# Decode attention in one step of a hybrid decoder: scores for two page groups per matmul, pages laid in pairs, a third sample's pages loaded in the stage before

## What is computed

```python
# 8 samples, 8 heads, 2048 past positions in 16 pages of 128; latent width 256, rotary width 32
ckv_past = cache_ckv[layer, page_table].reshape(b, -1, KV_LORA)
kpe_past = cache_kpe[layer, page_table].reshape(b, -1, QK_ROPE)
q_lat = jnp.einsum('bshd,chd->bshc', q_nope, p['w_uk'])
sc_past = jnp.einsum('bshc,btc->bhst', q_lat, ckv_past) + jnp.einsum('bshr,btr->bhst', q_pe, kpe_past)
...
pr = jax.nn.softmax(sc, axis=-1).astype(ckv.dtype)
o_lat = (jnp.einsum('bhst,btc->bshc', pr[..., :n_past], ckv_past)
         + jnp.einsum('bhst,btc->bshc', pr[..., n_past:], ckv))
return jnp.einsum('bshc,chd->bshd', o_lat, p['w_uv']).reshape(b, s, A_HEADS * V_DIM)
```

## Time and profile before

| what | value |
|---|---|
| three runs | 1036.63, 1037.03, 1031.61 us (median 1036.63) |
| profiled execution, first to last instruction | 1035.9 us |
| PE busy in it | 946.9 us |
| prompt attention block, decode attention block | about 217 to 255 us, about 255 to 338 us |
| granted TensorE clock, mean | 0.961 |

### The profile page before, as it was taken

One profiled execution on the slowest core, in us unless ns is written; L12 is line 12 of the kernel. 1 busy time (PEld: TensorE's weight loads), 2 busy tenths in 40 slices (PEclk: granted clock), 3 DMA queues, 4 the chain that ended last, 5 costly groups with the idle time before them and its releaser, 6 DMA issues. The chain is left out here.

```text
span 1035.9 us, 18712 instructions
## 1 busy us (share of the span) xinstructions
PE 946.9 (91%) x7761; PEld 583.3 (56%) x7761; DVE 340.8 (33%) x840; ACT 192.5 (19%) x461; POOL 120.2 (12%) x148
## 2 busy tenths in 40 slices
PE   4599999998998688999599999999999999999996
PEld 3488888876555456855554544454445454444451
DVE  0323660046344874525522322221121222212124
ACT  1010010325222591003111111110111111111102
POOL 0000000041563000000001101101011111101000
PEclk8899999998999787999889999999999999999998
DMA  9947575543796848076569999999999999999951
GB/s 376 318 173 289 206 313 204 204 164 128 255 346 215 344 172 347 11 280 256 222 222 405 426 421 419 417 420 418 398 405 423 420 423 421 421 421 398 401 196 50
DMA packets 56023, 319.87 MB, mean 309 GB/s; under 512 B 14929, under 2 KB 24738, under 8 KB 35010
## 3 DMA queue, kind: packets, MB, share of 16 engines
q1 hardware_dynamic: 43138, 300.20, 72.2%
q0 software_dynamic: 11072, 18.28, 5.2%
q10 hardware_dynamic: 1728, 0.18, 0.1%
HBM read 321.32 MB, written 15.77 MB: 325 GB/s over the span
## 5 line engine op out<-in xcount | busy, mean ns | idle before, releaser
L390 PE MATMUL bank<-h,ring 128*128 128x264 f32 x672 | 154.9, 391 | 9.7 <-PEq L306 9.1
L390 PEld LDWEIGHTS bank<-h,ring 128*128 128x128 f32 x672 | 128.1, 192 | 33.9 <-issue 12.2
L2315 DVE TENSOR_TENSOR hh<-sge,bank 64x256 f32<-64x256 f32 x64 | 27.1, 423 | 231.1 <-ACT sge L2226 231.1
L2226 ACT ACTIVATE sge<-bank 64x256 f32<-64x256 f32 x64 | 24.1, 377 | 416.7 <-PE bank L2108 416.7
L2108 PE MATMUL bank<-done_out,xt 128*64 128x256 f32 x832 | 95.6, 382 | 0.0
L2108 PE MATMUL bank<-ring,xt 128*64 128x256 f32 x800 | 94.9, 391 | 0.8 <-ACT xt L2217 0.8
L2262 DVE COPY sq<-bank 128x512 f32<-128x512 f32 x64 | 44.3, 692 | 110.7 <-PE bank L2049 107.5
L2049 PE MATMUL bank<-ring,ht 128*32 128x512 f32 x400 | 72.8, 598 | 3.2 <-DMA ring<-in_w_e 1.8
L1542 POOL DMA_INDIRECT xg<-tok_rows,tab_g x32 | 31.9, 998 | 375.2 <-PE bank L2035 342.5
L2108 PEld LDWEIGHTS bank<-done_out,xt 128*64 128x64 f32 x832 | 58.6, 138 | 27.1 <-issue 0.2
L2108 PEld LDWEIGHTS bank<-ring,xt 128*64 128x64 f32 x800 | 57.7, 142 | 28.6 <-issue 3.3
(11 more groups left out here) (462 smaller groups left out, 1194.7 us busy)
## 6 DMA issues: line engine op xcount, KB each, us to landing
ring<-in_w_units SPq DMA_DIRECT2D x28, 2048.0 KB, 10.6
done_out<-in_w_e SPq DMA_DIRECT2D x26, 2048.0 KB
ring<-in_w_e SPq DMA_DIRECT2D x25, 2048.0 KB
slot_b<-in_w_e SPq DMA_DIRECT2D x13, 2048.0 KB
ring<-in_w_e SPq DMA_DIRECT2D x25, 1024.0 KB
slot_b<-in_w_e SPq DMA_DIRECT2D x13, 1024.0 KB
done_out<-in_w_e SPq DMA_DIRECT2D x13, 1024.0 KB
row_of<-in_w_e SPq DMA_DIRECT2D x13, 1024.0 KB, 16.4
```

The lines of the kernel that those rows point to most:

```text
L390: mm = pe.matmul(bank[:, t % NB, 0:T], w[:, j, k, :], h[:, k, :], start=(k == 0), stop=(k == KD - 1))
L2226: act.activation(sg[e % 2][:, :], bank[0:LB, 4, 0:FE], ACT.Silu).then_inc(sg_ready, 1)
L2315: dve.tensor_tensor(hh[e % 2][:, :], sg[e % 2][:, :], bank[LB:2 * LB, 4, 0:FE], ALU.mult).then_inc(hh_ready, 1)
```

## The change

`held_turned` holds page 2 of samples 3 to 7 turned for m = 0 and 1 instead of m = 0 and 2. Two neighbouring groups make a pair. For each pair `score_pair` takes one matmul of 256 columns where `score_group` took two of 128; its moving operand spans both groups (a slice of two in the page buffer, or `page_t`, now laid out as 5 slots of a pair's two turned pages). TensorE's order becomes: turns of groups 0 and 1; turns of groups 2 and 3, scores of the first pair, `turn_weights` of sample b - 1; scores of the second pair; `weigh` of sample b - 1. VectorE takes all its copies of sample b before the probabilities of sample b - 1. In the prompt block `kh` now lies in `x`, and `val`, `t2` and `q_rows` in `sq`; with that memory free, SP and POOL issue the loads of three samples there (`range(NBUF)`) and begin with sample 3 in the decode block.

```diff
@@ -40,7 +40,7 @@
-    return g == 3 or (g == 2 and (b < FULL or m % 2 == 0))
+    return g == 3 or (g == 2 and (b < FULL or m < 2))
@@ -49,6 +49,13 @@
+PAIRS = {}
+for _b in range(TS):
+    for _h in range(NPG // 8):
+        for _g in range(4):
+            if not held_turned(_b, 2 * _h, _g):
+                PAIRS[_b, _h, _g] = len(PAIRS)
+NPAGE_T = 5
@@ -572,17 +579,19 @@
-    own = ExitStack()
-    kh = sb("kh", [QH, NH, TP], stack=own)
-    val = sb("val", [P, 2, NH * VD], stack=own)
+    page.append(page2)
+    rope.append(rope2)
+    kh = x[0:QH, :, 0:TP]
+    spare = sq[:, :, :].rearrange("p k t -> p (k t)")
+    val = spare[:, 0:2 * NH * VD].rearrange("p (t c) -> p t c", t=2)
...
-        t2 = sb("t2", [P, 2, T], stack=ph)
+        t2 = spare[:, 2 * NH * VD:2 * NH * VD + 2 * T].rearrange("p (a t) -> p a t", a=2)
...
-        q_rows, q_turned = sb("q_rows", [P, 2 * KVL], stack=ph), sem("q_turned", ph)
+        q_rows, q_turned = spare[:, 2 * NH * VD + 2 * T:2 * NH * VD + 2 * T + 2 * KVL], sem("q_turned", ph)
@@ -600,18 +609,19 @@
-                for b in range(NBUF - 1):
+                for b in range(NBUF):
...
-                for b in range(NBUF - 1):
+                for b in range(NBUF):
@@ -778,16 +788,8 @@
-    own.close()
...
-        page.append(page2)
-        rope.append(rope2)
-        page_t = early[:, 0:16 * P].rearrange("p (n i t) -> p n i t", n=8, i=2)
+        page_t = early[:, 0:4 * NPAGE_T * P].rearrange("p (s i m t) -> p s i m t", s=NPAGE_T, i=2, m=2)
@@ -827,7 +829,7 @@
-                for b in range(NBUF - 1, TS):
+                for b in range(NBUF, TS):
@@ -836,46 +838,51 @@
-                    pg = page[b % NBUF]
...
-                    for m in range(GR + 1):
-                        if m < GR:
...
-                        if b and m == 2:
+                    for h in range(GR // 2 + 1):
+                        if h < GR // 2:
+                            turn_pages(b, 2 * h)
+                            turn_pages(b, 2 * h + 1)
+                        if h >= 1:
+                            score_pair(b, h - 1)
+                        if b and h == 1:
...
-                def score_group(b, m):
-                    n = max(TURNS[b, m, g] for g in range(4) if not held_turned(b, m, g))
+                def turn_pages(b, m):
+                    pg = page[b % NBUF]
+                    pe.wait_ge(page_in[b % NBUF][m], 16 * 3 * (b // NBUF + 1))
+                    pe.wait_ge(fourth_in[b % NBUF][m], 16 * 2 * (b // NBUF + 1))
+                    for g in range(4):
+                        if held_turned(b, m, g):
+                            continue
+                        n = TURNS[b, m, g]
+                        if n >= 4:
+                            pe.wait_ge((turn_took_a, turn_took_d)[n % 2], (n - 4) // 2 + 1)
+                        for i in range(2):
+                            at = page_at(g) + i * P
+                            mm = pe.transpose(bank[:, n % 4, i * P:(i + 1) * P], pg[:, m, at:at + P], ident)
+                        mm.then_inc(turned, 1)
...
+                def score_pair(b, h):
+                    n = max(TURNS[b, 2 * h + 1, g] for g in range(4) if not held_turned(b, 2 * h + 1, g))
...
+                    ms, cols = slice(2 * h, 2 * h + 2), slice(2 * h * P, (2 * h + 2) * P)
...
-                            if held_turned(b, m, g):
+                            if held_turned(b, 2 * h, g):
...
-                                keys = page[b % NBUF][:, m, at:at + P]
+                                keys = page[b % NBUF][:, ms, at:at + P]
...
-                                keys = page_t[:, TURNS[b, m, g] % 8, i, :]
-                            pe.matmul(bank[32 * g:32 * g + 32, 4 + b % 2, m * P:(m + 1) * P], q_lat[:, i, b, :], keys,
+                                keys = page_t[:, PAIRS[b, h, g] % NPAGE_T, i, :, :]
+                            pe.matmul(bank[32 * g:32 * g + 32, 4 + b % 2, cols], q_lat[:, i, b, :], keys,
...
-                        mm = pe.matmul(bank[on_g, 4 + b % 2, m * P:(m + 1) * P], q_rot[on_g, b, :], rope[b % NBUF][on_g, m, :],
+                        mm = pe.matmul(bank[on_g, 4 + b % 2, cols], q_rot[on_g, b, :], rope[b % NBUF][on_g, ms, :],
...
-                    if m == GR - 1:
+                    if h == GR // 2 - 1:
@@ -944,7 +951,7 @@
-                            copy(page_t[:, n % 8, :, :], bank[:, n % 4, 0:2 * P].rearrange("p (a c) -> p a c", a=2)).then_inc(done, 1)
+                            copy(page_t[:, PAIRS[b, m // 2, g] % NPAGE_T, :, m % 2, :], bank[:, n % 4, 0:2 * P].rearrange("p (a c) -> p a c", a=2)).then_inc(done, 1)
@@ -984,10 +991,9 @@
-                    take_pages(dve, dve.tensor_copy, b, 1, turn_took_d, range(0, 3))
+                    take_pages(dve, dve.tensor_copy, b, 1, turn_took_d)
...
-                    take_pages(dve, dve.tensor_copy, b, 1, turn_took_d, range(3, GR))
```

More of the change, by code:

```diff
@@ L602, in pair_scores @@
                         return bank[:, 2 + 2 * half:4 + 2 * half, :].rearrange("p b (h k) -> p (b h) k", k=TP)
+                    assert nc.sbuf_base <= HI - 4 * GR * (PW + PAGE)
                     with nc.Block() as block:
@@ L799, in build @@
                     lat_rows = prob[0]
-                    pick = early[:, 16 * P:16 * P + TS * 32].rearrange("p (b h) -> p b h", h=32)
-                    rest = early[0:TS, 18 * P:]
+                    pick = early[:, 4 * NPAGE_T * P:4 * NPAGE_T * P + TS * 32].rearrange("p (b h) -> p b h", h=32)
+                    rest = early[0:TS, 4 * NPAGE_T * P + TS * 32:]
                     taken = [0]
@@ L838, in score_pages @@
                             def score_pages(b):
-                                pg = page[b % NBUF]
                                 if b >= 2:
                                     pe.wait_ge(exp5, b - 1)
-                                for m in range(GR + 1):
-                                    if m < GR:
-                                        pe.wait_ge(page_in[b % NBUF][m], 16 * 3 * (b // NBUF + 1))
-                                        pe.wait_ge(fourth_in[b % NBUF][m], 16 * 2 * (b // NBUF + 1))
-                                        for g in range(4):
-                                            if held_turned(b, m, g):
[L848 to L857, removed]
-                                    if b and m == 2:
-                                        turn_weights(b - 1)
```

## The result

| | before | changed |
|---|---|---|
| median of six runs | 1036.83 us (1031.61 to 1038.46) | 1045.14 us (1039.36 to 1048.95) |
| ratio to before | | 1.0067, 95% interval 1.0039 to 1.0094 |
| span of the profiled execution | 1035.9 us | 1047.0 us (a run of 1048.68) |
| from W(6) to the end of the span | 707.8 us | 707.8 us |

The change makes the kernel slower by 0.67%. The profiled execution (mean granted clock 0.950) lies at the upper end of the six runs, so its 11 us are more than the median's 8: the three slowest runs have a mean clock of 0.950 to 0.951, the three fastest 0.959 to 0.961, where the profiled execution of before has 0.961.

A forecast was written before the change was run, and what follows sets the result against it. Decode attention was taken as paced by a loop of release, page landing, remaining scores and weighing. Landing +0.8 and clock falls +3.6 gave +4.4 us on the 1036.6 us median: 1041.0 us, own range 1037.5 to 1045.

The forecast's parts named there:

- W(6): End of weighing sample 6, the decode attention's last changed point: 328.12 us before, 328.9 forecast without clock falls.
- rival 3: Decode attention: loads spread, landings at 13.8 us and 2.2 us a clock fall, +10.1 us, 1046.7 us; chance 0.17.
- The loop sets the pace: Decode attention: release, landing of pages, rest of scores, weighing and next release pace two samples, 19.4 us before.
- 6.3 us behind the last landing instead of 4.8: Samples 3 to 7: turns 0.75, pair 1.56, `turn_weights` 0.59, pair 1.56, weighing 1.87 follow the fourth group's landing.
- The stall, its place and its releaser: PE idles 2 us or more before turns of groups 2 and 3 in samples 3, 5, 7, no engine named.
- L = 12.9: Samples 3 to 7: time from buffer release to the last group's landing, 12.9 us, between 11.5 and 14.4.
- 1.2 us for a fall of the clock: Samples 3, 5 and 7: 3 us of work at 0.6 speed loses 1.2 each, +3.6 us, bounds 0 and 7.
- W(0): End of weighing sample 0 in the decode attention: forecast at 271.3 us, 1.3 us earlier than 272.63.
- Third load ahead 0: Sample 2's load issued in the prompt block: priced at 0, from -0.5 to +0.5 us.
- no more pages turned: `held_turned` edit: 74 turns before and after, 8 for samples 0 to 2 and 10 for the others; nothing to price.
- Rival 2: Decode attention TensorE-bound if pages land within some 10 us: 8.3 us a sample, -7.5 us, 1029.1 us; chance 0.15.
- Rival 1: Decode attention landing-bound while the clock holds: +0.8 us, 1037.4 us; chance 0.22.

The follow-up runs named there:

- x_norope: The changed kernel without the indirect DMAs of the rotary keys for samples 3 to 7: 0.9994 of the kernel before, median 1037.2 us.
- the release kernels: Five kernels giving the buffer back per page group, on the changed kernel, variants of it and the kernel before: 0.9969 to 1.0008 of the kernel before.
- x_order: The changed kernel with the first pair scored and the previous sample's probabilities turned before groups 2 and 3 are turned: 1.0006 of the kernel before, median 1040.1 us.
- a_rel: The changed kernel with the buffer given back per page group and nothing else: 1.0008 of the kernel before, median 1039.4 us.
- a_tiny: The changed kernel with page loads of samples 3 to 7 cut to one partition and no rotary loads for them: 0.9919 of the kernel before.
- x_filler: The changed kernel with four extra identity transposes before each wait for groups 1, 2 and 3 of samples 3, 5, 7: 1.0009 of the kernel before, median 1039.7 us.
- x_ahead: The kernel before with only the moved prompt-block tensors and the third sample's load issued there: 0.9988 of the kernel before.

## Why the prediction was right, and where its sizes were off

The prediction had the direction and the mechanism: a loop of release, landing and remaining work, made longer behind the landing, with a clock that falls in the wait. Of the size it had about half: 4.4 us forecast, 8.3 between the medians, 11.1 between the profiled executions. The 1045.14 us lie just above its own range of 1037.5 to 1045. The sizes are those of rival 3, which had a chance of 0.17: it gave landings of 13.8 us and 2.2 us a fall, hence cycles of 22.3 us, W(6) at 338.2 and 1046.7 us; measured are 13.6 to 14.2 us, 2.1 us a fall on average, cycles of 22.4, 22.7 and 21.8 us, and W(6) at 339.2. Its reason for the late landings, loads that share the engines with the next one, was not tested by itself.

- **The loop sets the pace**: right. x_norope shortens the landing, the release kernels bring the release forward, and x_order takes work from behind the landing; the stage follows each time (69.2, 68.8 for a_rel, 73.7 us against 80.8). a_tiny shows what is there without the loop.
- **6.3 us behind the last landing instead of 4.8**: right. a_tiny's row gives pair + probabilities + pair + weighing from 288.53 to 294.11 = 5.58, and with 0.75 of turns 6.3; x_filler and a_rel measure 6.4.
- **The stall, its place and its releaser**: right for groups 2 and 3 of samples 3, 5 and 7, where PE stands 2.2, 2.0 and 3.3 us; in three of these six waits the trace names the landing itself, in the others nothing. That group 1 would be late as well (1.41 us in sample 3) was missed.
- **L = 12.9**: too short. 14.2, 13.6 and 13.9 were measured, 2.9 us more in sum. It was read from loads whose successor came 9 us later; now it comes 7.6 us later, which may be a part of it and is not shown. x_norope shows that the indirect DMAs, by POOL's issue time or their small packets, are a part of L. L also varies by itself: x_filler has 13.1 us in sample 3, with the same loads and releases.
- **1.2 us for a fall of the clock**: the term that was mis-sized most in proportion: 1.9, 2.8 and 1.6, or 6.3 us instead of 3.6. I let a fall cover 3 us at 0.6 of the speed. Behind the landings the lower level lasted 3.9, 6.1 and 3.4 us, and a pair ran at 0.54 of its speed (1.56 us of work in 2.88).
- **W(0)**: 13.9 us after sample 0's start against 14.1 worked out. In the trace it stands 1.1 us later than forecast, because the stage begins 1.3 us later (258.45 against 257.16). Most of that is there long before: the transposes at the end of the projection block start at 204.58 before and here at

```profile
205.55 1.04 PE L411 MATMUL bank<-con,raw 128*128 128x128 f32 x8
```

  which is ahead of the change's first instruction. Over all profiled executions the stage begins between 256.1 and 258.7 us, on kernels with and without the change, so this shift is not the change's.
- The sum: 332.5 was forecast for W(6) with the falls, 339.2 came. 1.1 from the start, 2.9 from L, 2.7 from the clock make the 6.7. They account for this one execution; the median run is faster.
- **Third load ahead 0, moved tensors 0, no more pages turned**: right; ratio 0.9988 for x_ahead.
- Rival 2 (TensorE-bound) is what a_tiny would be, 8.09 us a sample; it needed the landings at 10 us, and they came at 13.6 to 14.2. Rival 1 (the clock holds) is what x_filler and a_rel show, not the change.
- The Trainium skill (DMA: Bandwidth & Descriptors, "Anatomy of one DMA") has 2.0 us plus bytes over 436 GB/s for a single DMA; taken for the 20 DMAs of a sample as if they were one, that estimate was 8.8 us, and the trace disagrees with 13.6 to 14.2 us.

## What to carry to other kernels

Where buffers come back late, as here, time saved on TensorE ahead of the last landing is worth nothing: ask of a reordering what it leaves to be done behind that landing, before asking what it saves. A batch that needs more inputs at once than the one it replaces moves its last input to the head of the work. And a stall that the kernel could afford becomes dear once the clock falls in it: here 3.4 to 6.1 us of the work behind each of three waits (3.4 to 3.8 us in sum, in pieces) ran at 1.2 GHz. The cheapest cure was to give buffers back in smaller pieces.

## What was not expected of the hardware

Extra transposes in the wait made the kernel faster by about 6 us. POOL's indirect DMAs, 64 KB of a load of 2.95 MB, held its landing back by 1.5 to 3 us. A load alone on the DMA engines took nearly as long as one among others: sample 2's 3.21 MB in the kernel before 11.5 to 13.5 us, the 2.95 MB of the changed kernel 13.6 to 14.2. A release up to 1.4 us earlier took 12 us off the stage of the changed kernel (80.8 to 68.8), and with it went the falls of the clock, in the profiled execution; some of that is chance, since with the same release the landing varied from 12.0 to 13.6 us.
